# Expert weights split into two float32r parts: pieces of 2048 elements per partition where there were pieces of 1024

## The reference, cut to what matters

```python
def _moe(h, router_w, router_bias, w_gate, w_up, w_down):
    scores = jax.nn.sigmoid((h @ router_w).astype(jnp.float32))
    ...                                    # comb: weights of the two chosen experts, 0 elsewhere
    for e in range(N_EXPERTS):             # 16
        he = jax.nn.silu(h @ w_gate[e]) * (h @ w_up[e])      # gate, up: 1024 x 256 each
        y = y + comb[:, e:e + 1] * (he @ w_down[e])          # down: 256 x 1024
    return y
```

## Time and profile before

| what | value |
|---|---|
| median of three runs | 1363.27 us |
| profiled execution, its own time | 1363.95 us |
| its span in the trace | 1362.1 us |
| busy: TensorE, VectorE, ScalarE | 1139.7, 857.4, 492.2 us (84, 63, 36% of the span) |
| mean granted TensorE clock | 0.916 of full speed |
| expert stage of layer 0, from the first WH piece to the last YO | 298.9 to 585.3 us |
| expert stage of layer 1, likewise | 1081.8 to 1339.5 us |
| WL pieces / WH pieces | 204 / 204, so 51 slots' weights are split |

### The profile page before, as it was taken

How to read it: one execution, slowest core, us unless ns; L and a number is a source line. 1 busy time by engine, 2 the same in 40 slices (tenths; PEclk the granted TensorE clock), 3 DMA queues, 4 the chain that set the end, 5 groups by cost and what they waited for, 6 DMA issues and landing times.

```text
span 1362.1 us, 16376 instructions
## 1 busy us (share of the span) xinstructions
PE 1139.7 (84%) x4753; PEld 827.9 (61%) x4754; DVE 857.4 (63%) x1008; ACT 492.2 (36%) x670; POOL 186.9 (14%) x126
## 2 busy tenths in 40 slices
PE   4969998638988999937999999978996389889992
PEld 1554445326666767726888888847874267667761
DVE  4775736366898879935444444444564669688882
ACT  5120112125555656643111111113121247466661
POOL 2000000022222324300000000000000013233331
PEclk9979998858998999968999999988998589999996
DMA  8547712415998898860133333430124168999855
GB/s 351 185 185 286 267 50 108 176 45 188 314 310 292 282 336 235 244 185 16 47 108 108 108 108 108 153 155 31 62 109 174 57 235 279 306 290 318 293 130 154
DMA packets 81619, 251.66 MB, mean 185 GB/s; under 512 B 8604, under 2 KB 33380, under 8 KB 72676
## 3 DMA queue, kind: packets, MB, share of 16 engines
q1 hardware_dynamic: 60180, 182.86, 35.4%
q0 software_dynamic: 17056, 50.40, 15.9%
q10 hardware_dynamic: 4336, 17.83, 3.4%
HBM read 220.65 MB, written 46.14 MB: 196 GB/s over the span
## 4 chain that ended last, share of the span: by engine, by line
PE 69%; DVE 13%; DMA 5%; ACT 4%; issue 4%; DVEq 1%; ACTq 1%; SPq 1%; POOL 0%; POOLq 0%
PE PS L1581 15%; PE PS L1488 7%; PE PS L1513 7%; PE PS L1685 7%; PE PS L1684 7%; PE PS L1688 7%; PE PS L1594 4%; PE PS L1600 3%; DMA RAW<-in_moe_w_up_dram 3%; PE PS L1525 2%; PE PS L1426 2%; PE PS L1571 2%; DVE WL L1223 2%; ACT WH L695 2%; DVE ACC L893 2%
## 5 line engine op out<-in xcount | busy, mean ns | idle before, releaser
L1223 DVE TENSOR_TENSOR WL<-RAW,WH 128x1024 fp32r<-128x1024 f32 x204 | 239.9, 1219 | 44.9 <-ACT WH L695 44.6
L695 ACT ACTIVATE WH<-RAW 128x1024 fp32r x204 | 203.9, 1053 | 120.7 <-issue 73.3
L1581 PE MATMUL PS<-WH,XTH 128*128 128x512 f32 x384 | 160.5, 418 | 22.6 <-issue 11.9
L1581 PE MATMUL PS<-WH,XTL 128*128 128x512 f32 x384 | 156.9, 409 | 0.0
L1581 PE MATMUL PS<-WL,XTH 128*128 128x512 f32 x384 | 156.7, 408 | 0.0
L1684 PE MATMUL PS<-HTH,WINH 128*128 128x512 f32 x384 | 151.8, 395 | 5.3 <-DVE HTL L1339 5.3
L1685 PE MATMUL PS<-HTL,WINH 128*128 128x512 f32 x384 | 153.2, 399 | 0.0
L480 POOL DMA_INDIRECT x_dram<-YO,TOKI x46 | 95.1, 2068 | 296.7 <-DVE YO L1237 150.5
L893 DVE SCALAR_TENSOR_TENSOR ACC<-WA,SC,ACC 128x1024 f32<-128x1024 f32 (+1 forms) x88 | 112.9, 1283 | 16.5 <-DMA WA<-in_w_ada_dram 12.0
L1688 PE MATMUL PS<-HTH,WINL 128*128 128x512 f32 x384 | 120.9, 396 | 0.0
L1488 PE MATMUL PS<-WF,FT 128*128 128x512 f32 x256 | 112.6, 600 | 2.1 <-DVE FT L963 2.1
(11 more groups left out here) (204 smaller groups left out, 1629.4 us busy)
## 6 DMA issues: line engine op xcount, KB each, us to landing
WA<-in_w_ada_dram SPq DMA_DIRECT2D x36, 1024.0 KB, 7.9
RAW<-in_moe_w_gate_dram SPq DMA_DIRECT2D x32, 1024.0 KB
RAW<-in_moe_w_up_dram SPq DMA_DIRECT2D x32, 1024.0 KB
WDR<-in_moe_w_down_dram SPq DMA_DIRECT2D x32, 1024.0 KB
WINR<-in_conv_w_in_dram SPq DMA_DIRECT2D x24, 512.0 KB, 3.7
x_dram<-X POOLq DMA_DIRECT2D x16, 512.0 KB, 2.9
h_dram<-H SPq DMA_DIRECT2D x16, 512.0 KB, 2.6
WA<-in_w_ada_dram ACTq DMA_DIRECT2D x8, 1024.0 KB, 9.7
```

The lines of the kernel that those rows point to most:

```text
L695: nc.scalar.activation(piece_of(WH[par], i), raw_piece(e, i), ACT.Copy).then_inc(w_high, 1)
L1223: V.tensor_tensor(piece_of(WL[par], i), raw_piece(e, i), piece_of(WH[par], i).bitcast(f32), ALU.subtract).then_inc(w_low, 1)
L1581: ins = T.matmul(bank(2), x[:, ch, :], w[par][:, :, ch, :], start=ch == 0 and i == 0, stop=ch == NC - 1 and i == 2)
```

## The change: two pieces of 2048 elements in place of four of 1024

PIECES becomes 2, and a piece now covers PART = 4 of the 8 chunks. Pieces 0 and 1 become piece 0, pieces 2 and 3 become piece 1, each at the place where the pair stood. `gate_up` waits at chunks 0 and 4. The expected counts follow.

```diff
-    PIECES = 4
+    PIECES = 2
+    PART = NC // PIECES
     def piece_of(t, i):
-        return t[:, :, 2 * i:2 * i + 2, :].rearrange("p j c f -> p j (c f)")
+        return t[:, :, PART * i:PART * (i + 1), :].rearrange("p j c f -> p j (c f)")
...
     def raw_piece(e, i):
-        return RAW[:, ds(e & 1, 1), :, 2 * i:2 * i + 2, :].rearrange("p r j c f -> p (r j) (c f)")
+        return RAW[:, ds(e & 1, 1), :, PART * i:PART * (i + 1), :].rearrange("p r j c f -> p (r j) (c f)")
...
             def slot(s, par):
                 down_high(s - 1)
-                weights_high(s + 1, 1 - par, (2, 3))
+                weights_high(s + 1, 1 - par, (1,))
                 gate(s)
                 xt_high(s + 1)
-                weights_high(s + 2, par, (0, 1))
+                weights_high(s + 2, par, (0,))
...
                 down_low(s - 1, e0)
-                weights_low(s + 1, 1 - par, e1, (2, 3))
+                weights_low(s + 1, 1 - par, e1, (1,))
                 gated(s, par)
                 xt_low(s + 1)
-                weights_low(s + 2, par, e2, (0, 1))
+                weights_low(s + 2, par, e2, (0,))
                 y_evac(s - 1, 1 - par, free)
...
                 for ch in range(NC):
-                    if ch % 2 == 0:
-                        pe.wait_ge(w_low, s * PIECES + (b0 * PIECES + ch // 2 + 1))
+                    if ch % PART == 0:
+                        pe.wait_ge(w_low, s * PIECES + (b0 * PIECES + ch // PART + 1))
```

More of the change, by code:

```diff
@@ L732, in _ @@
             xt_high(1)
-            weights_high(2, 0, (0, 1))
+            weights_high(2, 0, (0,))
             if layer == 0:
@@ L746, in _ @@
                 with act.Else():
-                    act.wait_ge(w_high, 2 * PIECES * i + ((b + 3) * PIECES - 2))
+                    act.wait_ge(w_high, 2 * PIECES * i + ((b + 3) * PIECES - 1))
                     for sig in (silu_g, xt_act, het_high, het_full):
@@ L753, in _ @@
                 down_high(MAX_SLOTS - 3)
-                weights_high(MAX_SLOTS - 1, 0, (2, 3))
+                weights_high(MAX_SLOTS - 1, 0, (1,))
                 gate(MAX_SLOTS - 2)
@@ L760, in _ @@
             with act.Else():
-                act.wait_ge(w_high, 2 * PIECES * PAIR_LOOPS + ((b + 3) * PIECES - 2))
+                act.wait_ge(w_high, 2 * PIECES * PAIR_LOOPS + ((b + 3) * PIECES - 1))
                 act.sem_inc(silu_g, 2)
                 act.sem_inc(xt_act, 1)
-                act.sem_inc(w_high, 2)
+                act.sem_inc(w_high, 1)
                 act.sem_inc(het_high, 3)
@@ L1257, in _ @@
             xt_low(1)
-            weights_low(2, 0, expert_of(2), (0, 1))
+            weights_low(2, 0, expert_of(2), (0,))
             for s in (1, 2):
@@ L1297, in _ @@
                     if s + 1 < MAX_SLOTS:
-                        weights_low(s + 1, 1 - s % 2, expert_of(s + 1), (2, 3))
+                        weights_low(s + 1, 1 - s % 2, expert_of(s + 1), (1,))
                     if s < MAX_SLOTS:
@@ L1307, in _ @@
                     dve.sem_inc(sig, 3)
-                dve.sem_inc(w_low, 2)
+                dve.sem_inc(w_low, 1)
                 dve.sem_inc(he_ready, 2)
```

## The result

The changed kernel took 1369.07 us (median of 20 runs, 1363.10 to 1381.56). The kernel before took 1363.03 us on the same chip (20 runs, 1358.68 to 1366.54). The ratio is 1.0050, with a 95% interval from 1.0031 to 1.0070. The profiled execution has a span of 1369.4 us and took 1371.22, where before had 1362.1 and 1363.95. So the sign is firm. The medians give 4 to 6 us, and the two intervals together allow 2.7 to 9.5.

What follows compares the result with a forecast made beforehand. It saw four regimes: TensorE without gaps, VectorE-bound at 341 to 443 us, weight loads, and ScalarE-to-VectorE crossings. Its terms (-0.76 at starts, the rest losses) sum to +4.4 us, giving 1367.6 us, range 1361.0 to 1372.0.

Steps and rivals of the forecast that it cites:

- The mechanism: Pairs handed from ScalarE's WH to VectorE's WL late, at some eight places: a net loss, chance 0.58.
- Removed work: 102 of 204 operations go on each engine; in unbroken runs a pair gains 0.06 us on VectorE, 0.09 on ScalarE.
- my first rival: Merged operations give their isolated saving, 0.15 and 0.20 us per pair: faster, 1360.8 or even 1348 us; chance 0.13.
- Layers' starts: Start of both layers: ScalarE's eight pieces take 7.30 us instead of 7.68, so the first product comes 0.38 earlier, twice.
- Late hand-over: Where ScalarE starts after a load, VectorE waits for the whole piece; what stands behind starts 0.76 us later.
- 341 to 443 us: VectorE-bound stretch of 16 WL pairs: two wait for ScalarE at 0.76 each, fourteen gain 0.06 each; sum +0.7 us.
- The load of 456.78 and the place at 503 us: Late pair delays the load's release and landing, +0.7; at 503.35 us YO is late and XTL moves, +0.4.
- 552 us: Late pair moves XTL and the product, +0.3, and TensorE's pipeline drains, +0.2; together +0.5 us.
- Ends of the layers: The last slot's YO stands behind a late WL pair, and the scatter waits for YO: +0.76 per layer, +1.5 in all.
- Layer 1, +0.76 at 1209.72 and +0.6 elsewhere: TensorE waits for YO behind a late hand-over at 1209.72 us, +0.76; three more late hand-overs near the chain, +0.6.
- TensorE-bound slots: Slots where TensorE has no gap: time without waits stays 9.8 us, since VectorE's waits for XTH take the delay in.
- the much slower rival: Nearly every first pair of a TensorE-bound slot becomes late, costing 0.25 to 0.3 us each: 1376 us; chance 0.07.

Runs made afterwards that it cites:

- e9: Kernel before, all operations of 1024, but VectorE waits for both high pieces for pieces 0 and 1 only: 1367.99 us against 1361.84, ratio 1.0047.
- e10: Kernel before, all operations of 1024, but VectorE waits for both high pieces for pieces 2 and 3 only: 1362.62 us against 1361.84, ratio 0.9999.
- e2: Changed kernel with pieces 0 and 1 single again, only 2 and 3 merged: 1360.10 us against 1363.06 of the kernel before, ratio 0.9980.
- e3: Changed kernel with pieces 0 and 1 merged, 2 and 3 single again: 1361.79 us against 1363.06 of the kernel before, ratio 0.9996.
- e11: The kernel of e3 timed once more in another series: 1363.12 us against 1361.84 of the kernel before, ratio 1.0012.
- e7: Kernel before, but SyncE issues an expert's load only after the other buffer's has landed: 1362.39 us against 1363.05, ratio 1.0000.
- e6: Changed kernel loading only two of eight gate and up chunks from each layer's third expert on: 1340.55 us against 1363.05 of the kernel before, ratio 0.9825.
- e1: The changed kernel timed again without edit: 1366.76 us against 1363.06 of the kernel before, ratio 1.0038.
- e8: Changed kernel, but SyncE issues an expert's load only after the other buffer's has landed: 1366.60 us against 1363.05 of the kernel before, ratio 1.0030.
- e4: Kernel before, all operations of 1024, but VectorE waits for the second high piece in every pair: 1367.13 us against 1363.06, ratio 1.0028.
- e12: The kernel of e2 with YO of the last slot moved between WL pieces 0 and 1: 1360.81 us against 1361.84 of the kernel before, ratio 0.9994.

## Why the prediction was right, and where it was not

The forecast was +4.4 us, with a chance of 0.43 for slower and 0.48 for no change that can be told; measured are +6.0 and, again, +3.7. (1363.27 + 4.4 is 1367.7, and the 1367.6 of the forecast is a slip.) The mechanism, a late hand-over of the pair behind XTL that costs where a load has just landed, is what e9 and e10 show, and e2 agrees; e3 and e11 have the hand-over without the loss, so it isn't the whole account. By its steps:

- **Removed work.** The operations are 102 of 2287 ns and 102 of 1915 ns, and the run of four WH takes 7.31 us, so the gain per pair on ScalarE is 0.09 us, as forecast. In the VectorE-bound stretch the slots of 12.0 and 12.2 us became 11.9 and 12.1: 0.1 per slot of two pairs, as 2 x 0.06 says. The isolated saving of 0.15 and 0.20 us, my first rival, appears nowhere. Right. For VectorE that saving is what the Trainium skill's "VectorE: DVE Perf Modes", section on the TRN2 errata, would lead to, by which the fixed time is exposed between instructions; the steps of this case's runs show 0.06 us.
- **Layers' starts, -0.38 each.** Found in both: XTH 7.21 us after the first WH in each, against 7.59, and the first product 0.36 and 0.38 us earlier. Right. That the clock behind it moves the start by 2 to 3 us from one execution to the next I hadn't seen.
- **Late hand-over, 0.76.** ScalarE to YO is 4.35 us at the landings against 3.55, so 0.8. VectorE's start moved from 1.28 to 2.13 us behind ScalarE. Right. The idle time ended by WH rose to 78.5 us with 39 waits; I had asked for 70 or more and about 40.
- **341 to 443 us, +0.7.** The count of late and early pairs was right, the sum was not. I took it that what a slot gains stays gained. The landing of the load didn't follow its release (2.38 us earlier issued, 0.98 earlier there), so the slot at 414 us grew by 2.3 us, where I had 0.76. Most of that lead was the clock's, though, and against e7 and e10, which had it too, the slot grew by 0.9 or 1.0 us. What failed is that I took the slots' gains as kept: here, an earlier issue of a load gave back only part of its lead.
- **The load of 456.78 and the place at 503 us, +0.7 and +0.4.** ScalarE starts at 504.25 in place of 503.35, so the landing is 0.9 us later, and XTL behind it is 1.27 us late. The shift ahead of it was -0.80 us at 468 us, because of the early product at 319, so the growth over these places is 2.1 us where I had 1.1. Here the sign was right and the size too small by half.
- **552 us, +0.5.** XTL went from 561.30 to 562.83, 1.53 us late, but it had been 2.18 and 1.65 us late at 531 and 541 us. The place itself cost nothing more. Wrong, by 0.5. The 0.2 in it for TensorE's drain is shown by no run; what the runs show behind long waits for YO is a granted clock of 0.50 to 0.58, which cost 0.66 us at 1215 us.
- **Ends of the layers, +0.76 each.** In layer 0 the last YO is 2.71 us late where the last XTL was 1.65: +1.06. In layer 1 it is 7.06 against 6.88: +0.18. In both the last WL starts 2.14 or 2.15 us after ScalarE, so the hand-over is as forecast. What blurs it is ScalarE's own start: it is 0.2 us late behind XTH at both ends, where before it was on time in layer 0 and 0.81 us late in layer 1. The sum was 1.5 and came out as 1.24.
- **Layer 1, +0.76 at 1209.72 and +0.6 elsewhere.** XTL is 3.2 us late at 1173 us, 5.4 at 1213 and 7.0 at 1305. I wrote that what is lost ahead of saturated loads is absorbed. It was not: WH of the four load-bound slots came 3.5, 4.7, 2.8 and 4.6 us later than before. TensorE's waits for YO ahead of the down product grew from 6.7 to 11.5 us over the whole kernel, but they don't measure the loss: they are 10.0 in e2, the fastest kernel, and 5.8 in e9. This is the term that was mis-sized most, 1.4 us forecast and 4.1 measured (XTL of the first slot is 2.7 us late, of the last 6.9), though how much of it belongs to the change and how much to the alternation of the slots can't be told from one execution of each.
- **TensorE-bound slots, nothing.** They stay 9.8 us, and e6 shows it without landings. Right; the much slower rival falls.

That the sum came so near is in part luck. Behind the third XTL the terms for layer 0 made +3.1 us (0.7, 0.7, 0.4, 0.5 and 0.76), those for layer 1 +2.1 (0.76, 0.76 and 0.6). The changed kernel's two profiled executions lost 4.5 and 2.8 us there in layer 0, and 4.3 and 1.8 in layer 1.

Layer 0 gives the cleanest measure of the effect, from its third XTL to its last YO, over the profiled executions with full loads and VectorE's order of before. The four with a fine late pair (before, e2, e7, e10) take 255.0 to 257.6 us, 256.1 in the mean. The seven with a coarse one all take longer. The five with merged operations (after, e1, e3, e8, e11) take 257.8 to 260.4, 259.3 in the mean and 3.2 us more, though e1 and e10 lie within 0.2 us of each other. The two in which only the wait is coarse (e4, e9) take 262.3 and 263.0, 6.6 us more than the fine ones. So the wait alone costs more there than the merge does, and e9's 6.2 us can't be taken as the price of the change. In layer 1 the three means are 224.7, 225.7 and 223.6 us, with a spread from 220 to 230: its time is set by the pattern of the load-bound slots, which no experiment controlled. What layer 1 adds to the loss, and why e3 and e11 have so little of it in all, isn't settled.

## What to carry to other kernels

When two operations on one engine feed a second engine, merging them moves the second engine's start by the time that the first takes for the second half (here from 1.28 to 2.14 us). Price that at each place where the first engine starts late (here 0.8 us behind a landing), against a saving read from an unbroken run of operations (here 0.06 us), not from their durations. Merge the group that is produced well ahead, and leave fine the one that is consumed at once: e2 does it, and among the kernels with all their loads it is the only one whose interval lies below before's time (0.9980 [0.9962, 0.9999]), if barely. That e3, the other half alone, is level with before warns that such a price isn't paid in every arrangement. Before reading a few us out of two profiles, compare the clock at the start of each stage. And don't count an earlier issue of a load as an earlier landing while other loads are in its queue.

## What the runs showed of the hardware that I had not expected

- A load of 2 MB (gate and up) issued 2.4 us earlier was there 1.0 us earlier at 414 us. In layer 1's stretch, whose DMA share is 0.94 in both kernels and 1.01 in e3, the time from issue to landing was 13.1 us before and 13.9 after, and 10.0 in e3, for the same expert.
- The same four slots ran as 11.3, 14.4, 11.4, 14.1 us or as 11.2, 11.3, 11.5, 11.7 in kernels whose work there differs by tenths of a us. Making SyncE issue the loads in turn (e8) didn't end the alternation.
- Reading a number of the routing from memory into a register took 0.26 to 1.64 us in the traces of before and after, on VectorE, ScalarE and SyncE, with medians of 0.27 to 0.31. The long ones are larger than one late hand-over, and in e12 they made three slots 1.3 us longer.
- TensorE's second product of a layer, with the same operations of TensorE ahead of it, ran at a granted clock of 1.00 in one execution and began at 0.50 in another (5.83 and 7.34 us at 319 us). In layer 1 the first two products took 7.37 and 5.83 us in e1, and 8.57 and 7.38 before. This moved a stage by 2 to 3 us, as much as the change itself.
